# RWKV units: inverted diagonal blocks stored without zeros and transposed by VectorE, output products reordered

## The reference, cut to what matters

```
for each chunk c, head h:            (T = 128 tokens, width 64)
  P = A S + (strictly lower part of A K^T) V        right side
  (I - strictly lower part of A B^T) U = P          solve
  Y = R S + (lower part of R B^T) U + (lower part of R K^T) V
  S = decay * (S + B^T U + K^T V)
```

## Time and profile before

| | us |
|---|---|
| runs, median of 3 | 3781.59 (3776.4, 3781.59, 3781.95) |
| profiled execution, its own time | 3777.6 |
| its span, first to last instruction | 3775.8 |
| TensorE busy | 3623.8 (96%) |
| VectorE busy | 1686.9 (45%) |
| ScalarE busy | 1496.5 (40%) |
| GpSimd busy | 1276.0 (34%) |

### The profile page before, as it was taken

The page is one execution under the profiler, slowest core; times in us unless marked ns, Lnnn a source line. Parts: engine busy times, 40 slices in busy tenths (PEclk is TensorE's granted clock), DMA queues, the critical chain, the costliest instruction groups (busy, mean ns, idle before and its releaser), DMA issues.

```text
span 3775.8 us, 47922 instructions
## 1 busy us (share of the span) xinstructions
PE 3623.8 (96%) x17684; PEld 2853.3 (76%) x17684; DVE 1686.9 (45%) x2392; ACT 1496.5 (40%) x2452; POOL 1276.0 (34%) x583
## 2 busy tenths in 40 slices
PE   8999999999999999999999998999999999999997
PEld 7877787888788777778877676888744588767886
DVE  2633457443345443754335643503347554536042
ACT  3256633332323664333325544423224244344232
POOL 4422233444443212434443242444200011433442
PEclk9999999999999999999999999999999999999999
DMA  3421122223233111222232221222322200222222
GB/s 138 127 65 49 46 78 75 98 94 106 88 101 113 50 45 57 90 84 95 100 101 95 100 91 60 95 96 99 102 83 74 72 2 29 95 67 84 96 99 78
DMA packets 100867, 313.06 MB, mean 83 GB/s; under 512 B 26208, under 2 KB 26336, under 8 KB 99808
## 3 DMA queue, kind: packets, MB, share of 16 engines
q1 hardware_dynamic: 81792, 298.90, 23.6%
q10 hardware_dynamic: 18912, 11.88, 1.3%
HBM read 302.35 MB, written 5.24 MB: 81 GB/s over the span
## 4 chain that ended last, share of the span: by engine, by line
issue 45%; PE 36%; POOL 16%; DVE 1%; DMA 1%; ACT 1%; POOLq 0%; DVEq 0%; SPq 0%; ACTq 0%
POOL ring_r L2734 16%; PE ps L456 9%; PE ps L458 9%; PE ps L457 9%; PE ps L964 2%; PE ps L1064 1%; PE ps L802 1%; PE ps L983 1%; DMA ring<-in_weights 1%; PE ps L1109 0%; PE ps L1147 0%; PE ps L1100 0%; PE ps L1149 0%; PE ps L1209 0%; PE ps L1208 0%
## 5 line engine op out<-in xcount | busy, mean ns | idle before, releaser
L2734 POOL TENSOR_TENSOR ring_r<-ring,rounded_r 128x1024 fp32r<-128x1024 f32 x504 | 1238.8, 2461 | 2032.2 <-ACT rounded_r L1254 2031.9
L456 PE MATMUL ps<-source_hi,rounded_r 128*128 128x512 f32 x2560 | 1019.2, 398 | 63.2 <-DVE N_lo L2312 23.6
L1254 ACT ACTIVATE rounded_r<-ring 128x1024 fp32r<-128x1024 f32 x504 | 533.6, 1059 | 1308.2 <-PE ps L458 1182.8
L457 PE MATMUL ps<-source_hi,ring_r 128*128 128x512 f32 x2560 | 1006.6, 393 | 0.0
L456 PEld LDWEIGHTS ps<-source_hi,rounded_r 128*128 128x128 f32 x2560 | 487.1, 190 | 179.2 <-DVE N_lo L2312 29.7
L458 PE MATMUL ps<-X_lo,rounded_r 128*128 128x512 f32 x1536 | 602.3, 392 | 0.0
L457 PEld LDWEIGHTS ps<-source_hi,ring_r 128*128 128x128 f32 x2560 | 487.3, 190 | 100.7 <-issue 1.7
L458 PEld LDWEIGHTS ps<-X_lo,rounded_r 128*128 128x128 f32 x1536 | 291.3, 190 | 62.0
L458 PE MATMUL ps<-N_lo,rounded_r 128*128 128x512 f32 x768 | 302.7, 394 | 0.0
L2277 DVE SCALAR_TENSOR_TENSOR T<-ps,PAR,T 128x511 f32<-128x511 f32 (+1 forms) x176 | 131.5, 749 | 229.1 <-ACT T L1469 214.2
L456 PE MATMUL ps<-H_hi,rounded_r 128*128 128x512 f32 x512 | 199.2, 389 | 0.0
(11 more groups left out here) (502 smaller groups left out, 5508.3 us busy)
## 6 DMA issues: line engine op xcount, KB each, us to landing
ring<-in_weights SPq DMA_DIRECT2D x560, 512.0 KB, 3.3
X<-in_x SPq DMA_DIRECT2D x2, 1024.0 KB, 7.0
PAIR<-Z ACTq DMA_DIRECT2D x32, 64.0 KB
out_x<-X SPq DMA_DIRECT2D x4, 512.0 KB, 2.6
SWAP<-Z ACTq DMA_DIRECT2D x4, 256.0 KB, 5.9
MEM<-in_mem ACTq DMA_DIRECT2D x1, 1024.0 KB, 4.8
mem_keys<-Z ACTq DMA_DIRECT2D x1, 1024.0 KB, 3.9
diag_in<-Y ACTq DMA_DIRECT2D x8, 128.0 KB, 2.2
```

What stands on the lines that cost most here:

```text
L456: mm(o, lh, rh, start=start, stop=False)
L457: mm(o, ll, rh, start=False, stop=False)
L1254: av(RH[:, j, :], ring[:, j, :], ACT.Copy).then_inc(w_hi, 1)
L2734: nc.gpsimd.tensor_tensor(RL[:, j, :], ring[:, j, :], RH[:, j, :].bitcast(F32), ALU.subtract).then_inc(w_lo, 1)
```

## The change

X0 is kept without zeros: 32 columns a head in place of 128, so that GpSimd writes it with one instruction a unit in place of four. The transposes leave TensorE: `turn_blocks` and ScalarE's `x0_turned` are gone, and VectorE transposes X0 from SBUF into `xt` with four instructions of 32 partitions a unit (`blocks_turned`), right behind the masks of the first grams. `xt` now has 64 columns a head: a row's own block beside the block that `inverse` adds; its zero blocks are set by VectorE for the first two units alone. The waits on `g1m` and `x0` that stood in `turn_blocks` move to `blocks_below`. Beside this, two orders on TensorE change: `turn_output(u-1)` comes ahead of `lower_half(u)`, and `outputs(u)` issues the products that don't need the solution first and waits for it (`ubc`) only then.

```diff
-        X0 = Y[:, 8, :].rearrange("p (q t) -> p q t", q=QU)
+        X0 = Y[:, 8, 0:QU * SUB].rearrange("p (q t) -> p q t", q=QU)
...
-                xt=xt.rearrange("p (q t) -> p q t", q=QU), bktok=...
+                xt=xt[:, 0:QU * HD].rearrange("p (q t) -> p q t", q=QU), bktok=...
...
-            def turn_blocks(u):
+            def blocks_below(u):
 
                 B, o, n0, t, c = unit(u)
                 pe.wait_ge(rw["g1m"], u + 1)
                 pe.wait_ge(rw["x0"], u + 1)
                 for q in range(QU):
-                    ins = nc.tensor.transpose(ps[:, o + 2, q * P:q * P + P], X0[:, q, :], cst("ident"))
-                ins.then_inc(rw["xt0"], 1)
-
-            def blocks_below(u):
-
-                B, o, n0, t, c = unit(u)
-                for q in range(QU):
                     for b in (0, HD):
                         ins = mm(ps[b + SUB:b + HD, o + 3, q * SUB:q * SUB + SUB], B["g1"][b:b + SUB, q, 1, b + SUB:b + HD],
-                                 X0[b:b + SUB, q, b:b + SUB], start=True, stop=True)
+                                 X0[b:b + SUB, q, :], start=True, stop=True)
                 ins.then_inc(rw["z"], 1)
...
             def outputs(u):
 
                 B, o, n0, t, c = unit(u)
-                pe.wait_ge(rw["ubc"], u + 1)
                 for n in range(2):
                     mm(ps[:, o + n, 0:P], AR[:, 0, n0 + n, t], B["sh"][:, n].rearrange("p h i -> p (h i)"), start=True, stop=False)
                     for h in range(2):
-                        y = ps[:, o + n, h * HD:h * HD + HD]
-                        mm(y, B["g1"][:, 2 * n + h, 0, :], PU[:, 1, 2 * n + h, :], start=False, stop=False)
-                        ins = mm(y, B["g2"][:, 2 * n + h, 0, :], B["vtok"][:, n, h * HD:h * HD + HD], start=False, stop=h == 1)
+                        mm(ps[:, o + n, h * HD:h * HD + HD], B["g2"][:, 2 * n + h, 0, :], B["vtok"][:, n, h * HD:h * HD + HD], start=False, stop=False)
+                pe.wait_ge(rw["ubc"], u + 1)
+                for n in range(2):
+                    for h in range(2):
+                        ins = mm(ps[:, o + n, h * HD:h * HD + HD], B["g1"][:, 2 * n + h, 0, :], PU[:, 1, 2 * n + h, :], start=False, stop=h == 1)
                 ins.then_inc(rw["y"], 1)
...
                 to_lower_half(u)
                 if after:
-                    turn_blocks(u + 1)
                     blocks_below(u + 1)
-                lower_half(u)
                 if u >= 1:
                     turn_output(u - 1)
+                lower_half(u)
                 if after:
                     inverse(u + 1)
                 outputs(u)
...
+            def blocks_turned(u):
+                B, o, n0, t, c = unit(u)
+                xt = B["xt"]
+                if u < 2:
+                    for b in (0, HD):
+                        v.memset(xt[b + SUB:b + HD, :, 0:SUB], 0.0)
+                else:
+                    dve.wait_ge(rw["ub"], u - 1)
+                dve.wait_ge(rw["x0"], u + 1)
+                for b in range(P // SUB):
+                    rows, at = slice(b * SUB, b * SUB + SUB), b % 2 * SUB
+                    ins = v.transpose(xt[rows, :, at:at + SUB], X0[rows])
+                ins.then_inc(rw["xt0c"], 1)
...
             masked(0, 2, "g1", "mask1", "g1", "g1m")
+            blocks_turned(0)
             masked(0, 0, "g2g", "mask2", "g2", "g2m")
...
                     masked(u + 1, 2, "g1", "mask1", "g1", "g1m")
+                    blocks_turned(u + 1)
...
                 if u >= 1:
                     pool.wait_ge(rw["z"], u)
-                for b in range(P // SUB):
-                    rows = slice(b * SUB, b * SUB + SUB)
-                    ins = nc.gpsimd.tensor_tensor(X0[rows, :, rows], DIAG[c][rows, h:h + QU, :],
-                                                  cst2("lower")[rows].unsqueeze(1).to_broadcast([SUB, QU, SUB]), ALU.mult)
-                ins.then_inc(rw["x0"], 1)
+                    pool.wait_ge(rw["xt0c"], u)
+                nc.gpsimd.tensor_tensor(X0, DIAG[c][:, h:h + QU, :], cst2("lower").unsqueeze(1).to_broadcast([P, QU, SUB]),
+                                        ALU.mult).then_inc(rw["x0"], 1)
```

More of the change, by code:

```diff
@@ L354, in build @@
                 g2=g2.rearrange("p k s -> p (k s)").rearrange("p (q a t) -> p q a t", q=QU, a=2),
-                xt=xt.rearrange("p (q t) -> p q t", q=QU), bktok=bktok.rearrange("p (a n c) -> p a n c", a=2, n=2),
+                xt=xt[:, 0:QU * HD].rearrange("p (q t) -> p q t", q=QU), bktok=bktok.rearrange("p (a n c) -> p a n c", a=2, n=2),
                 vtok=CSF[:, L * 256:L * 256 + 256].rearrange("p (n c) -> p n c", n=2),
@@ L414, in build @@
             "lora_a", "g2", "exp", "hat", "gram", "ext", "cut", "out0", "out1", "in", "solved", "back", "diag", "r", "prod", "bonus", "bv", "bias",
-            "tr", "tok", "g1", "g1m", "x0", "g2g", "g2m", "xt0", "xt0c", "z", "zc", "xt1", "xt1c", "sh", "p", "pt", "ut", "utc", "pb",
+            "tr", "tok", "g1", "g1m", "x0", "g2g", "g2m", "xt0c", "z", "zc", "xt1", "xt1c", "sh", "p", "pt", "ut", "utc", "pb",
             "pbc", "ub", "ubc", "y", "yc", "center", "sq", "var", "root", "yn", "yt", "out", "hi", "s", "st")}
@@ L1137, in inverse @@
                     for b in (0, HD):
-                        ins = mm(ps[b:b + SUB, o + 2, q * SUB:q * SUB + SUB], ZI[b + SUB:b + HD, q, :], B["xt"][b + SUB:b + HD, q, b + SUB:b + HD],
+                        ins = mm(ps[b:b + SUB, o + 2, q * SUB:q * SUB + SUB], ZI[b + SUB:b + HD, q, :], B["xt"][b + SUB:b + HD, q, SUB:HD],
                                  start=True, stop=True)
@@ L1165, in upper_half @@
                 for q in range(QU):
-                    ins = mm(ps[0:HD, o + 2, 2 * P + q * HD:2 * P + q * HD + HD], B["xt"][0:HD, q, 0:HD], PU[0:HD, 0, q, :], start=True, stop=True)
+                    ins = mm(ps[0:HD, o + 2, 2 * P + q * HD:2 * P + q * HD + HD], B["xt"][0:HD, q, :], PU[0:HD, 0, q, :], start=True, stop=True)
                 ins.then_inc(rw["ut"], 1)
@@ L1184, in lower_half @@
                 for q in range(QU):
-                    ins = mm(ps[HD:P, o + 2, 2 * P + q * HD:2 * P + q * HD + HD], B["xt"][HD:P, q, HD:P], PU[HD:P, 0, q, :], start=True, stop=True)
+                    ins = mm(ps[HD:P, o + 2, 2 * P + q * HD:2 * P + q * HD + HD], B["xt"][HD:P, q, :], PU[HD:P, 0, q, :], start=True, stop=True)
                 ins.then_inc(rw["ub"], 1)
@@ L1219, in _ @@
             key_grams(0)
-            turn_blocks(0)
             blocks_below(0)
@@ L1855, in tokens_copied @@
                 av(B["vtok"].rearrange("p n c -> p (n c)"), ps[:, o + 1, 0:2 * P], ACT.Copy).then_inc(rw["tok"], 1)
[L1857 to L1860, removed]
             def below_copied(u):
@@ L1875, in inverse_copied @@
                 for b in (0, HD):
-                    ins = av(B["xt"][b:b + SUB, :, b + SUB:b + HD], x[b:b + SUB], ACT.Copy)
+                    ins = av(B["xt"][b:b + SUB, :, SUB:HD], x[b:b + SUB], ACT.Copy)
                 ins.then_inc(rw["xt1c"], 1)
@@ L1912, in _ @@
             tokens_copied(0)
-            x0_turned(0)
             below_copied(0)
@@ L1931, in _ @@
                 if after:
-                    x0_turned(u + 1)
                     below_copied(u + 1)
@@ L2755, in _ @@
             pool.wait_ge(rw["hat"], KT)
-            nc.gpsimd.memset(X0, 0.0)
             for L in range(2):
```

## The result

| | us |
|---|---|
| changed kernel, median of 4 runs | 3824.59 (3818.04 to 3830.97) |
| kernel before, median of 4 runs | 3780.95 (3776.4 to 3781.95) |
| ratio | 1.0118, 95% interval 1.0102 to 1.0135 |
| profiled execution, its time and span | 3823.24, 3821.4 |

The change makes the kernel 44 us slower. The direction is the forecast's, the size is four times its +10.3 us and lies outside the range. The whole of it is in the units. From the first transposes of unit 0 (L1090, at 2982.12 before and 2985.51 after) to the first product behind the units (L456, at 3183.61 and 3229.82) it is 201.49 us before and 244.31 after, +42.8. I call this distance the stage from here on.

The account below looks back on a forecast made before the run. The prediction took TensorE, without slack, to bound the stage. Stalls of +11.6 us, -1.3 for unit 0, -0.6 for iteration 0 and +0.6 for the last gave +10.3 us, forecast as 3790 us, range 3779 to 3800.

Parts of the forecast that it names:

- The bound: In the units TensorE is busy throughout a 12.30 us iteration; turn_output's operand is ready 1.03 us before turn_output starts.
- Transposes on VectorE: Four VectorE instructions between the mask and output_low, 1.20 us an iteration, with bounds of 0.67 and 2.01 us.
- The stall: TensorE waits 1.41 us at turn_output for the norm in iterations 1 to 14: net +0.83 us each, +11.6 us together.
- Start and end: Unit 0 gains 1.3 us and iteration 0 gains 0.6; the last iteration costs 0.6, with lower_half behind turn_output.
- What costs nothing: Waits of outputs, ScalarE, GpSimd and VectorE's wait for ub: met in time, so priced at nothing.
- the later root: ScalarE's root comes 1.20 us later; the copy behind it ends at 3086.80, before lower_half wants it at 3088.7: no cost.
- The sum: Over the whole kernel, 11.6 - 1.3 - 0.6 + 0.6 = +10.3 us; the forecast case had a chance of 0.65.
- a fall of the clock: The clock in the units falling below 1.00 with the new gaps would show the forecast wrong; no size or chance given.
- the highest rival: Slower still: VectorE's transposes take 2.01 us an iteration, +21.7 us, 3801 us in all; chance 0.10.

Follow-up runs that it names:

- e7: The changed kernel with three useless identity transposes on TensorE in the place of its wait (iterations 1 to 14); 1.0036 of the kernel before.
- e6: The changed kernel with VectorE's four transposes moved behind the norm and output_low(u-2) behind them; 0.9989 of the kernel before.
- e10: e6 with lower_half ahead of turn_output in the last iteration alone; 0.9977 of the kernel before.
- e4: The kernel before with only the order of the products in outputs changed; 1.0003 of the kernel before.
- e3: The changed kernel with lower_half ahead of turn_output again; 1.0049 of the kernel before.
- e2: The changed kernel with nine useless identity transposes on TensorE in the place of its wait (iterations 1 to 14); 1.0033 of the kernel before.
- e9: e3 with three useless identity transposes on TensorE between turn_output and inverse, in no gap; 1.0017 of the kernel before.
- e11: The changed kernel with one useless identity transpose on TensorE in the place of its wait; 1.0115 of the kernel before.

## Why the prediction was right and wrong

- **The bound.** Right: TensorE without slack, and the slack of 1.03 us between norm and `turn_output` as the place where it is decided.
- **Transposes on VectorE.** Right: 1.20 us forecast from L1983 with the step to the next instruction, 1.27 measured (1.24 for the four alone). The four hardly overlap, 0.30 us each, as in that row.
- **The stall.** Right: 1.41 us forecast, 1.42 measured, 14 times. With the clock kept up (e7) an iteration takes 3082.44 - 3069.24 = 13.20 us; 13.13 was forecast.
- **Start and end.** Unit 0 and iteration 0 together gave 2.5 us (L1090 to the next iteration's `right_upper`: 3006.08 - 2982.12 = 23.96 before, 3006.95 - 2985.51 = 21.44 after) where 1.9 was forecast. The last iteration costs 0.8 (e6 against e10), 0.6 forecast.
- **What costs nothing.** Right for `outputs` (e4), ScalarE and GpSimd (one instruction of 0.46 us, far from the path), in the changed kernel. That the later root pushes ScalarE's copy was seen, and that it would matter in another order (e3) was not said.
- **The sum.** +10.3 us forecast; with the gap filled, the same order costs 11.1 us of stage and 12 us by the runs (e2: 1.0033). The sum was right for what it summed. A part of that is luck: 14 iterations at 13.21 us are 12.7 us and not 11.6, and the larger gain at the start (2.5 for 1.9) took most of the difference back.
- **The step that failed** is the one from a stall to its price. The prediction priced the idle time at its own length and took the durations of all other rows as fixed. They are not: they hold at a clock of 1.00. It named a fall of the clock only as a thing that would make it wrong, with no chance and no price, and the highest rival, +21.7 us, was again VectorE's. What the runs showed in its place: the same stall costs 11.1 us of stage when TensorE is kept busy in it (e2, clock 1.00) and 42.8 when it isn't (clock 0.86). What was missing is 31.7 us of stage, three quarters of the result. The Trainium skill (TensorE: Matmul & The Clock Gate, section on why this matters for your kernels) warns of idle gaps between bursts of products, and the gaps that it warns of are longer than any here; by that line alone these would have been harmless and the sum would have stood. The measurement decides: 1.17 and 1.42 us, once in each 13 us, brought the clock down, and in e3 so did 0.38 and 0.37.

What stays open is the rule by which the clock falls. e3 against e9 shows that gaps of equal length cost it or not by the work beside them, e7 against e11 that two filler transposes decide, which shorten the gap and add work at once. Nor is it known why of two neighbouring iterations with the same products and the same gap one ran at 1.00 and the next at 0.74. No run here tells whether columns, sizes of the products or their spacing count.

## What to carry to other kernels

Before work is put on an engine with spare time, find the stretch of its queue in which it would stand: half an engine's time may be idle and all of it in the wrong place. The same four instructions, moved by some lines to where VectorE waited anyhow, turn +44 us into -5 (0.13%). With the last late instruction behind them too, and `lower_half` first in the last iteration, the gain was 0.23% (e10), though the runs hardly tell these versions apart. Where TensorE runs dense chains of small products, as in this stage, new gaps of a microsecond or less are not priced by their length: compare the granted clock, and if in doubt fill the gap with useless transposes, which splits the wait's price from the clock's in one run.

## What the hardware showed

- Two filler transposes an iteration decided over the whole price of the clock: gap 0.95 us, stage +12 us and clock 1.00 (e7); gap 1.17 us, stage +47 us and clock 0.84 (e11).
- The fall came and went within one execution, with the gap in every iteration: 13.21 us at clock 1.00, 17.35 us at 0.74 in the next.
- Adding useless work on TensorE's own path made the stage shorter, 215.52 to 208.98 us (e3 to e9), because the clock stayed at 1.00 in place of 0.93.
- Four VectorE transposes of 32x32 blocks, 32 partitions x 128 float32 elements, took 1.24 us one partition quarter after the other, 0.30 each: as much as elementwise instructions of that shape, 1.19 for four.
